# Gated linear attention in a fused decoder block: block-diagonal state tiles, and the order of state update and output copy on the vector engine

## The chip, the cores and the metric

The kernel runs on one core of a Trainium2 chip. The core has a matrix engine (TensorE; PE in the profile, PEld its weight loads), a vector engine (VectorE, DVE), a scalar engine (ScalarE, ACT), GpSimd (POOL) and a queue engine for transfers (SyncE, SP). The metric is the device time of one execution in microseconds (us); the kernel before takes 2816.35 us in the median of three runs.

## The reference, cut to what matters

The kernel computes one decoder block over 2048 tokens of width 1024: a mixing stage (two head groups side by side, mLSTM and gated linear attention), cross-attention and an MLP, all in float32. The change is in the gated linear attention (GLA), which has 4 heads with keys of 64 and values of 128 channels:

```python
def gla_chunkwise(q, k, v, log_a):
    # S_t = diag(a_t) S_{t-1} + k_t v_t^T, o_t = q_t S_t
    def step(Sst, inp):
        qc, kc, vc, la = inp
        b = jnp.cumsum(la, axis=2)
        diff = jnp.where(causal[:, :, None], b[:, :, :, None, :] - b[:, :, None, :, :], -jnp.inf)
        A = jnp.einsum('bhtd,bhsd,bhtsd->bhts', qc, kc, jnp.exp(diff))
        o = (jnp.einsum('bhts,bhse->bhte', A, vc)
             + jnp.einsum('bhtd,bhde->bhte', qc * jnp.exp(b), Sst))
        bL = b[:, :, -1]
        kw = kc * jnp.exp(bL[:, :, None] - b)
        S_new = jnp.exp(bL)[..., None] * Sst + jnp.einsum('bhsd,bhse->bhde', kw, vc)
        return S_new, o
```

The output of a chunk has a part from inside the chunk (A times v) and a part carried by the state (q exp(b) times S). The state of a head is a 64 x 128 matrix.

## The kernel before, in words

The tokens are taken in four groups of 512 (the first three in a loop, the last written out), each of four chunks of 128. Within a group every engine walks the same list of steps s, one for each slab of weights (128 rows by 512 columns). A product with weights is split in three terms of high and low parts, so a slab is 12 matmuls of TensorE (L1981). ACT rounds a slab to its high part (`w_hi`, L905), DVE subtracts to get the low part (`w_lo`, L1419), TensorE waits for `slab_lo`. Between the slabs stand the small operations of the two attentions, at steps fixed by hand (`M_SLAB` = 25, `G_SLAB` = 41). Each engine runs its own list in order, and semaphores join them.

The GLA part of a group takes steps 41 to 53. Chunk c, counted from 0, has three steps beginning at 41 + 3c:

- In the first step TensorE runs `levels(c, (0, 1))` (L2097, L2100), in the second `side_even_heads` (L2109), `levels(c, (2, 3))` and `side_odd_heads`. `levels` makes the sums inside a chunk, in 64 x 64 tiles of the array; for each head DVE masks the result (L1564, signals `lvl_masked`) and sums it (L1568). `levels(c, (2, 3))` waits until DVE has masked heads 0 and 1 of the same chunk.
- In the first step of the chunk after it (steps 44, 47, 50, 53), ahead of that chunk's `levels`, TensorE finishes chunk c: `outputs_start` multiplies the weighted queries `qe` of heads 0 and 2 by the state `stS` (L2135); `state_step` makes the update of the state (L2166, signals `s_full`); `outputs` does heads 1 and 3 of the carried part (L2135), after a wait for its own first pair (`o_even`), and adds the part from inside the chunk (L2157, signals `o_full`).
- At the same steps DVE copies the output out of PSUM (L1744, waits for `o_full`, signals `o_out`), updates the state (two instructions, L1749, one for each pair of heads, waits for `s_full`), and goes on to the masks of the next chunk.

The state tile `stS` is 128 partitions by 2 by 128: heads 0 and 2 lie on partitions 0 to 63, heads 1 and 3 on partitions 64 to 127, each pair j in its own columns. So L2135 is a matmul over 64 rows, two for each pair of partitions, and both pairs add into the same bank of PSUM (`work[:, 2]`).

ACT waits at the same steps for `o_out`, squares the output head by head (L1226), and then goes on: at step 47 it loads a table and applies the sigmoid of the gate (L1240) before the next rounding L905; at step 53 it scales the turned mLSTM heads (L1099, `x_hi`), whose low part DVE makes (L1585, `x_lo`) for the first slab of the output projection, step 56. At step 49 DVE gates the four mLSTM heads (`gate_heads`, L1606, 16 instructions).

DVE and ACT instructions may start on a part of the partitions: L1632 subtracts on partitions 64 to 87 (`gT[low]`), L1625 clears partitions 64 to 127 of `a_full`.

The lines that say what a sentence can't:

```python
for hd in hds:                       # carried(c, hds), L2131 to L2137
    j, p0 = hd // 2, 64 * (hd % 2)
    ins = mm(work[:, 2, cut[hd]], qe[p0:p0 + 64, c % 2, j, :], stS[p0:p0 + 64, j, :],
             start=(hd == 0), stop=False, skip_group_check=True)
```

## Time and profile before

| | |
|---|---|
| median of 3 runs | 2816.35 us (2816.01 to 2817.10) |
| time of the profiled execution | 2816.63 us |
| its span, first to last instruction | 2815.1 us |
| granted TensorE clock, mean | 0.999 |
| TensorE busy | 2796.2 us (99%) |
| DVE busy | 1812.2 us (64%) |
| ACT busy | 1514.2 us (54%) |
| share of TensorE in the chain that ended last | 98% |

Columns of the timeline rows below: start in us from the span's start, time in us from the first start to the last end of the row, engine, line, operation, output and inputs by the program's names, shapes, number of instructions in the row, and in brackets idle time of the engine before it and what ended it. A float32 matmul shows as two records. The span of 1.1 us less than the profiled time is the part around the program. A busy matrix engine is not one that waits for nothing: ends of matmuls are modelled, and only the distance from start to start shows its pace.

### The profile page before, as it was taken

What the parts mean: (1) busy time and instruction counts of PE and PEld (TensorE: products, weight loads), DVE (VectorE), ACT (ScalarE), POOL (GpSimd) and SP (SyncE); (2) the same over time, 40 slices, a digit from 0 to 9 for tenths busy, and PEclk for the clock granted to TensorE, in tenths of its full rate; (3) what the DMA queues carried; (4) which work ended last, traced back from release to release, by engine and by line L of the source; (5) the groups of instructions that cost most, each with busy time, mean ns of one, the idle gap of its engine ahead of it and who ended that gap; (6) DMA issues with size and microseconds to landing.
All of it is one profiled execution on the core that took longest, in us unless ns stands there. A gap on an engine that the chain in (4) does not pass through costs nothing.

```text
span 2815.1 us, 44964 instructions
## 1 busy us (share of the span) xinstructions
PE 2796.2 (99%) x15076; PEld 2328.2 (83%) x15076; DVE 1812.2 (64%) x3011; ACT 1514.2 (54%) x3126; POOL 1054.5 (37%) x1334
## 2 busy tenths in 40 slices
PE   8999999999999999999999999999999999999998
PEld 8888888888878888888888888888888888888887
DVE  6376764776686755556788675466668675545665
ACT  6555444566655444555565544456655544455553
POOL 5264554665354400234546320044435550013330
PEclk9999999999999999999999999999999999999999
DMA  6732476565552222355554222255455222234442
GB/s 216 251 105 67 173 268 242 186 211 151 149 188 83 76 89 90 108 171 161 164 177 135 69 84 90 90 158 179 143 150 199 81 74 90 90 104 144 151 149 83
DMA packets 185906, 393.41 MB, mean 140 GB/s; under 512 B 14224, under 2 KB 14368, under 8 KB 185664
## 3 DMA queue, kind: packets, MB, share of 16 engines
q1 hardware_dynamic: 160112, 309.89, 35.2%
q0 software_dynamic: 22880, 75.72, 8.0%
q10 hardware_dynamic: 2672, 4.76, 0.5%
q8 instruction: 129, 2.11, 0.3%
q14 instruction: 113, 0.93, 0.1%
HBM read 346.24 MB, written 33.59 MB: 135 GB/s over the span
## 4 chain that ended last, share of the span: by engine, by line
PE 98%; DMA 1%; ACT 0%; DVE 0%; issue 0%; POOL 0%; ACTq 0%; DVEq 0%
PE bank L1981 44%; PE work L1981 22%; PE bank L2348 17%; PE work L2348 3%; PE work L1995 1%; PE bank L2386 1%; PE work L2097 1%; DMA vo_dram<-folded 1%; PE bank L1995 1%; PE work L2135 1%; PE work L2157 1%; PE work L2043 1%; PE work L2246 1%; PE work L2250 1%; PE work L2245 1%; PE work L2229 1%
## 5 line engine op out<-in xcount | busy, mean ns | idle before, releaser
L905 ACT ACTIVATE w_hi<-raw 128x512 fp32r<-128x512 f32 x1156 | 724.7, 630 | 1012.6 <-PE bank L1981 514.5
L1419 DVE TENSOR_TENSOR w_lo<-raw,w_hi 128x512 fp32r<-128x512 f32 x657 | 481.2, 736 | 785.8 <-ACT w_hi L905 784.2
L1417 DVE SCALAR_TENSOR_TENSOR w_lo<-raw,w_hi 128x512 fp32r<-128x512 f32 x499 | 448.8, 921 | 92.6 <-ACT w_hi L905 91.6
L737 POOL TENSOR_TENSOR hr<-qk 128x256 f32<-128x256 f32 x60 | 44.9, 750 | 773.3 <-ACT qk L1293 773.3
L2348 PE MATMUL bank<-w_hi,h_hi 128*128 128x512 f32 x720 | 280.3, 389 | 0.1
L2348 PE MATMUL bank<-w_hi,h_lo 128*128 128x512 f32 x720 | 280.1, 389 | 0.0
L2348 PE MATMUL bank<-w_lo,h_hi 128*128 128x512 f32 x720 | 280.1, 389 | 0.0
L1981 PE MATMUL bank<-w_hi,x_hi 128*128 128x512 f32 x640 | 255.2, 399 | 0.0
L1981 PE MATMUL bank<-w_lo,x_hi 128*128 128x512 f32 x640 | 249.6, 390 | 0.0
L1981 PE MATMUL bank<-w_hi,x_lo 128*128 128x512 f32 x640 | 249.5, 390 | 0.0
L727 POOL TENSOR_TENSOR h_lo<-qk,h_hi 128x256 fp32r<-128x256 f32 x180 | 180.7, 1023 | 71.1 <-ACT h_hi L1306 71.1
L1981 PE MATMUL work<-act_hi,w_hi 128*128 128x512 f32 x512 | 199.2, 389 | 0.0
L1981 PE MATMUL work<-act_lo,w_hi 128*128 128x512 f32 x512 | 199.2, 389 | 0.0
L1981 PE MATMUL work<-act_hi,w_lo 128*128 128x512 f32 x512 | 199.2, 389 | 0.0
L1981 PE MATMUL bank<-act_hi,w_hi 128*128 128x512 f32 x464 | 180.8, 390 | 0.0
L1981 PE MATMUL bank<-act_hi,w_lo 128*128 128x512 f32 x464 | 180.5, 389 | 0.0
L1981 PE MATMUL bank<-act_lo,w_hi 128*128 128x512 f32 x464 | 180.5, 389 | 0.0
L2348 PEld LDWEIGHTS bank<-w_hi,h_hi 128*128 128x128 f32 x720 | 135.1, 188 | 28.8 <-issue 0.7
L2348 PEld LDWEIGHTS bank<-w_hi,h_lo 128*128 128x128 f32 x720 | 135.1, 188 | 28.2
L2348 PEld LDWEIGHTS bank<-w_lo,h_hi 128*128 128x128 f32 x720 | 135.1, 188 | 27.9
L791 POOL TENSOR_TENSOR zz<-zz,gqkv 128x128 f32<-128x128 f32 x224 | 118.0, 564 | 106.8 <-ACT gqkv L1251 106.8
L1981 PE MATMUL bank<-x_hi,w_hi 128*128 128x512 f32 x384 | 152.9, 398 | 0.0
(405 smaller groups left out, 6465.0 us busy)
## 6 DMA issues: line engine op xcount, KB each, us to landing
raw<-in_w_dram SPq DMA_DIRECT2D x226, 512.0 KB, 3.9
raw<-sums_dram SPq DMA_DIRECT2D x120, 512.0 KB, 3.9
raw<-in_w_in_dram SPq DMA_DIRECT2D x112, 512.0 KB, 3.5
raw<-in_w_out_dram SPq DMA_DIRECT2D x32, 512.0 KB, 4.1
raw<-kq_dram SPq DMA_DIRECT2D x32, 512.0 KB, 3.8
raw<-vo_dram SPq DMA_DIRECT2D x32, 512.0 KB, 3.8
xres<-in_x_dram POOLq DMA_DIRECT2D x16, 512.0 KB, 5.9
early_rows<-in_w_dram POOLq DMA_DIRECT2D x8, 1024.0 KB, 8.8
```

Source lines behind the costliest of these rows:

```text
L727: nc.gpsimd.tensor_tensor(operand(q, h_lo)[:, kt, :], src, operand(q, h_hi)[:, kt, :].bitcast(F32), ALU.subtract).then_inc(operand_lo_pool, 1)
L737: nc.gpsimd.tensor_tensor(diff[:, kt, :], quarter(0, 0, kt), quarter(0, 1, kt), ALU.subtract).then_inc(diff_ready, 1)
L791: ins = nc.gpsimd.tensor_tensor(v[:, :, :, r, :], v[:, :, :, r, :], src, ALU.mult)
L905: nc.scalar.activation(w_hi[:, slot, :], raw[:, pair_slot, slot % 2, :], ACT.Copy).then_inc(slab_hi, 1)
L1417: ins = stt(out=w_lo[:, slot, :], in0=src, scalar=1.0, in1=hi, op0=ALU.mult, op1=ALU.subtract)
L1419: ins = tt(w_lo[:, slot, :], src, hi, ALU.subtract)
L1981: ins = mm(dst, left, right, start=(kt == 0 and j == 0), stop=(kt == KT - 1 and j == 2))
L1995: ins = transpose(into[kt % 4][:, i * P:(i + 1) * P], src[:, i, kt * P:(kt + 1) * P], ident[:])
L2043: ins = mm(wbank[2 + j % 2][:, hh * MEM:(hh + 1) * MEM], left, right, start=(k == 0 and i == 0), stop=(k == 1 and i == 2))
L2097: ins = mm(dst, z, z, start=True, stop=True)
L2135: ins = mm(work[:, 2, cut[hd]], qe[p0:p0 + 64, c % 2, j, :], stS[p0:p0 + 64, j, :], start=(hd == 0), stop=False, skip_group_check=True)
L2348: ins = mm(dst[:], left[:, kt, here], right[:, kt, :], start=(CHAIN_BEFORE[q] is None and kt == 0 and j == 0), stop=(kt == HALF - 1 and j ...
```

## The change

- The state tile becomes 128 partitions by 2 by 256, block-diagonal: of pair j, the even head's 64 x 128 block stands on partitions 0 to 63 in columns 0 to 127, the odd head's on partitions 64 to 127 in columns 128 to 255; the rest stays zero.
- So one matmul over all 128 rows makes the carried output of both heads of a pair (128 x 128 by 128 x 256). Both are issued in a row in `outputs_start`; the semaphore `o_even` and the second call of `carried` go.
- DVE updates the state before the output's copy, in four instructions on 64 partitions each, in the order of the heads: partitions 0, 64, 0, 64.
- Nine small tiles of four columns become one tile of ten rows, and the unused tile shrinks from 232 to 8 columns to make room.

```diff
-        stS = sb("stS", [P, 2, HD])
+        stS = sb("stS", [P, 2, 2 * HD])
...
                     if slot == 0 and 1 <= c <= NCH:
-                        dve.wait_ge(o_full, 4 * g + c)
-                        nc.vector.tensor_copy(tok[:, c - 1, COLS:], work[:, 2, :]).then_inc(o_out, 1)
                         dve.wait_ge(s_full, 4 * g + c)
                         if c >= 2:
                             dve.wait_ge(s_ready, 4 * g + c - 1)
-                        for j in range(2):
-                            ins = stt(out=stS[:, j, :], in0=stS[:, j, :], scalar=eb[:, (c - 1) % 2, j, CH - 1:CH],
-                                      in1=work[:, 3, j * HD:(j + 1) * HD], op0=ALU.mult, op1=ALU.add)
+                        for hd in range(HEADS):
+                            j, k, half = hd // 2, hd % 2, slice(64 * (hd % 2), 64 * (hd % 2) + 64)
+                            own = stS[half, j, k * HD:(k + 1) * HD]
+                            ins = stt(out=own, in0=own, scalar=eb[half, (c - 1) % 2, j, CH - 1:CH],
+                                      in1=work[half, 3, j * HD:(j + 1) * HD], op0=ALU.mult, op1=ALU.add)
                         ins.then_inc(s_ready, 1)
+                        dve.wait_ge(o_full, 4 * g + c)
+                        nc.vector.tensor_copy(tok[:, c - 1, COLS:], work[:, 2, :]).then_inc(o_out, 1)
...
-                def carried(c, hds):
-
-                    for hd in hds:
-                        j, p0 = hd // 2, 64 * (hd % 2)
-                        ins = mm(work[:, 2, cut[hd]], qe[p0:p0 + 64, c % 2, j, :], stS[p0:p0 + 64, j, :],
-                                 start=(hd == 0), stop=False, skip_group_check=True)
-                    return ins
+                def carried(c, j):
+
+                    return mm(work[:, 2, j * 2 * HD:(j + 1) * 2 * HD], qe[:, c % 2, j, :], stS[:, j, :],
+                              start=(j == 0), stop=False, skip_group_check=True)
...
                     stand_alone(pe)
-                    carried(c, (0, 2)).then_inc(o_even, 1)
+                    for j in range(2):
+                        carried(c, j)
...
                     pe.wait_ge(at_full, 4 * g + c + 1)
-                    pe.wait_ge(o_even, 4 * g + c + 1)
                     stand_alone(pe)
-                    carried(c, (1, 3))
```

On TensorE, where a chunk is finished (here at step 47), the order was as follows. The rows give the stationary operand's columns by the moving one's; `stS`, `kwT` and `sg` are the state, the turned weighted keys and the weights inside the chunk.

```order
L1981 MATMUL bank<-w_hi,x_lo 128x512
L2135 MATMUL work<-stS,qe 128x128 [waits o_out,o_ss]
L2135 MATMUL work<-stS,qe 128x128
L2166 MATMUL work<-gqkv,kwT 64x128 [waits side_out]
L2166 MATMUL work<-gqkv,kwT 64x128 x3
L2135 MATMUL work<-stS,qe 128x128 [waits at_full,o_even]
L2135 MATMUL work<-stS,qe 128x128
L2157 MATMUL work<-gqkv,sg 128x128 x4
```

With the change it is:

```order
L1975 MATMUL bank<-w_hi,x_lo 128x512
L2127 MATMUL work<-stS,qe 128x256 [waits o_out,o_ss]
L2127 MATMUL work<-stS,qe 128x256
L2156 MATMUL work<-gqkv,kwT 64x128 [waits side_out]
L2156 MATMUL work<-gqkv,kwT 64x128 x3
L2147 MATMUL work<-gqkv,sg 128x128 [waits at_full]
L2147 MATMUL work<-gqkv,sg 128x128 x3
```

Four matmuls of 128 columns over 64 rows became two of 256 columns over 128 rows, all of them ahead of the state's update.

On DVE, at steps 49 and 50, the order was:

```order
L1606 SCALAR_TENSOR_TENSOR qk<-tok,hscale,qk 128x128 x15
L1414 REGISTER_ALU
L1419 TENSOR_TENSOR w_lo<-raw,w_hi 128x512 [waits slab_hi]
L1744 COPY tok<-work 128x512 [waits o_full]
L1749 SCALAR_TENSOR_TENSOR stS<-stS,eb,work 128x128 [waits s_ready,s_full]
L1749 SCALAR_TENSOR_TENSOR stS<-stS,eb,work 128x128
L1562 REGISTER_ALU
L1564 TENSOR_TENSOR mw<-work,lvl_mask 128x448 [waits lvl_full]
```

With the change it is:

```order
L1598 SCALAR_TENSOR_TENSOR qk<-tok,hscale,qk 128x128 x15
L1406 REGISTER_ALU
L1411 TENSOR_TENSOR w_lo<-raw,w_hi 128x512 [waits slab_hi]
L1741 SCALAR_TENSOR_TENSOR stS<-stS,eb,work 64x128 [waits s_ready,s_full]
L1741 SCALAR_TENSOR_TENSOR stS<-stS,eb,work 64x128 x3
L1745 COPY tok<-work 128x512 [waits o_full]
L1554 REGISTER_ALU
L1556 TENSOR_TENSOR mw<-work,lvl_mask 128x448 [waits lvl_full]
```

The copy moved behind the state's update, and the update has four instructions instead of two, in front of the next mask in both.

## Rows read from the trace of the kernel before

**Rows 1.** The page: busy time, share of the span and instructions of each engine.
```profile
PE 2796.2 (99%) x15076; PEld 2328.2 (83%) x15076; DVE 1812.2 (64%) x3011; ACT 1514.2 (54%) x3126; POOL 1054.5 (37%) x1334
```

**Rows 2.** Timeline of PE at step 44 of the first group.
```profile
265.07 0.39 PE L1981 MATMUL bank<-w_hi,x_lo 128*128 128x512 f32 x1
265.39 0.71 PE L2135 MATMUL work<-stS,qe 64*128 64x128 f32 x4
266.03 0.66 PE L2166 MATMUL work<-gqkv,kwT 128*64 128x128 f32 x8
266.62 0.71 PE L2135 MATMUL work<-stS,qe 64*128 64x128 f32 x4
267.26 1.16 PE L2157 MATMUL work<-gqkv,sg 128*128 128x128 f32 x8
268.35 0.93 PE L2097 MATMUL work<-zz 64*64 64x64 f32 x48
```

**Rows 3.** Timeline of PE in the mLSTM part: from a slab into float32 matmuls.
```profile
223.65 0.39 PE L1981 MATMUL bank<-w_hi,x_lo 128*128 128x512 f32 x1
223.88 1.05 PE L2229 MATMUL work<-qk 128*128 128x128 f32 x8
224.76 0.60 PE L2233 MATMUL work<-ident,qk 128*128 128x128 f32 x4
```

**Rows 4.** Timeline of PE: `levels` of steps 47 and 48, 50 and 51.
```profile
282.86 0.93 PE L2097 MATMUL work<-zz 64*64 64x64 f32 x48
...
286.99 0.28 PE L2097 MATMUL work<-zz 64*64 64x64 f32 x3
...
297.37 0.93 PE L2097 MATMUL work<-zz 64*64 64x64 f32 x48
...
301.76 0.93 PE L2097 MATMUL work<-zz 64*64 64x64 f32 x48
```

**Rows 5.** Timeline of DVE, steps 48 to 51.
```profile
288.76 0.69 DVE L1419 TENSOR_TENSOR w_lo<-raw,w_hi 128x512 fp32r<-128x512 f32 x1 [1.57 <-ACT w_hi L905]
...
298.37 0.68 DVE L1744 COPY tok<-work 128x512 f32<-128x512 f32 x1
298.97 0.59 DVE L1749 SCALAR_TENSOR_TENSOR stS<-stS,eb,work 128x128 f32<-128x128 f32 x2
299.49 0.61 DVE L1564 TENSOR_TENSOR mw<-work,lvl_mask 128x448 f32<-128x448 f32 x1
...
301.00 0.62 DVE L1564 TENSOR_TENSOR mw<-work,lvl_mask 128x448 f32<-128x448 f32 x1
```

**Rows 6.** DVE busy in one window: its ends, length, busy time, instructions, clock, transfers.
```profile
288.76:301.62 12.86, 12.75 (x29) 1.00 0.26 83
```

**Rows 7.** Timeline of DVE in the second group: an instruction on partitions 64 to 87.
```profile
799.84 0.67 DVE L1419 TENSOR_TENSOR w_lo<-raw,w_hi 128x512 fp32r<-128x512 f32 x1
...
800.54 0.69 DVE L1632 TENSOR_TENSOR gT<-work,gT 24x512 fp32r<-24x512 f32 x1
```

**Rows 8.** Timeline of DVE: a clearing of partitions 64 to 127.
```profile
248.53 1.13 DVE L1618 SCALAR_TENSOR_TENSOR stC<-stC,bc,work 128x129 f32<-128x129 f32 x4
249.76 0.27 DVE L1625 MEMSET sg<- 64x256 f32 x1
```

**Rows 9.** Timeline of DVE at step 44: the output's copy.
```profile
268.45 0.69 DVE L1744 COPY tok<-work 128x512 f32<-128x512 f32 x1 [1.60 <-PE work L2157]
```

**Rows 10.** Timeline of ACT, steps 47 and 48.
```profile
284.86 1.28 ACT L1240 ACT_TABLE_LOAD   x1
286.15 2.07 ACT L1240 ACTIVATE qk<-bank 128x512 f32<-128x512 f32 x4
288.08 0.65 ACT L905 ACTIVATE w_hi<-raw 128x512 fp32r<-128x512 f32 x1
```

**Rows 11.** Timeline of DVE at step 54: the last low parts before the output projection.
```profile
318.35 1.42 DVE L1585 SCALAR_TENSOR_TENSOR x_lo<-tok,norm_g,x_hi 128x512 fp32r<-128x512 f32 x2 [0.20 <-ACT x_hi L1099]
```

**Rows 12.** Timeline of PE at step 56: the output projection's first matmul.
```profile
320.22 0.39 PE L1981 MATMUL work<-w_hi,x_hi 128*128 128x512 f32 x1
```

More of the change, by code:

```diff
@@ L111 @@
 PRO_ROWS = MEM // P + NCH
-SPARE = 232
+SPARE = 8
 N_SUMS = HB * HALF
@@ L217, in program @@
         stC = sb("stC", [P, HEADS, HD + 1])
-        stS = sb("stS", [P, 2, HD])
+        stS = sb("stS", [P, 2, 2 * HD])
         mrow = sb("mrow", [1, NCH + 1, HEADS])
-        ss = sb("ss", [P, NCH])
-        ss_b = sb("ss_b", [P, NCH])
-        var = sb("var", [P, NCH])
-        lnv = sb("lnv", [P, NCH])
-        y0 = sb("y0", [P, NCH])
-        y1 = sb("y1", [P, NCH])
-        rstd = sb("rstd", [P, NCH])
-        rs_attn = sb("rs_attn", [P, NCH])
-        rs_mlp = sb("rs_mlp", [P, NCH])
+        row_cols = sb("row_cols", [P, 10, NCH])
+        ss, ss_b, var, lnv, y0, y1, rstd, rs_attn, rs_mlp = (row_cols[:, k, :] for k in range(9))
         hss = sb("hss", [P, 2, NCH, HEADS])
@@ L402, in program @@
         at_full = sem("at_full")
-        o_even = sem("o_even")
         o_full = sem("o_full")
```

## The prediction

> **What bounds the kernel now.** I read the page first. TensorE is busy 99% of the span, DVE 64% [rows 1], so the kernel is TensorE's instruction stream, and a change pays by what it takes out of that stream, unless it makes TensorE wait. Then I read TensorE's timeline where a chunk is finished, from start to start. After the last matmul of a slab at 265.07 come the four L2135 records of heads 0 and 2 at 265.39, the state's update at 266.03, the four records of heads 1 and 3 at 266.62, the inner part at 267.26, and `levels` at 268.35 [rows 2]: 3.28 us for the whole passage. Last I asked who is close behind TensorE. In steps 47 and 48 the two calls of `levels` start 4.13 us apart, in steps 50 and 51 4.39 us [rows 4], though the same work stands between them: TensorE waits there for 0.26 us, once in each group. It waits for DVE's mask of head 1, which ends at 301.62 (301.00 + 0.62), and goes on at 301.76 [rows 4, 5]. DVE has no room there: from 288.76 to 301.62, 12.86 us, it is busy for 12.75 [rows 6]. So at this one place of the group DVE is the bound already, and the change gives DVE more to do.
>
> **What TensorE gains.** In one shape of the array, a float32 record with 128 moving columns takes 0.11 us from start to start (eight from 223.88 to 224.76), and the first starts 0.23 after a slab's last matmul [rows 3], which is the slab's own pace. The four L2135 records take 0.64 instead of 0.44, and the first starts 0.32 after the slab instead of 0.23 [rows 2]. So a passage from one tile shape (128x128, 64x128, 128x64) to another costs about 0.20 us, half as a late start, half on the first record behind it. Before there are four such passages up to L2157: slab to 64x128, to 128x64, to 64x128, to 128x128. After there are two. The removed wait for `o_even` costs nothing: the passage from the second L2135 to L2157, with no wait in it, costs as much as the one into it. The streaming stays the same, eight records of 0.11 against four with 256 columns. No row has a float32 record of 256 columns. It lies between twice 0.11, 0.22, and a slab's record, 0.23, which I read as streaming as long; I take 0.22, since the overhead of one record is in both. New passage: 0.23 + 3 x 0.22 + (0.22 + 0.09) + 0.59 for the state (266.03 to 266.62) + 1.09 for the inner part (267.26 to 268.35) = 2.88 us. Gain 0.40 us for each chunk (0.36 at the other bound), 16 chunks, 6.4 us if nothing else moves.
>
> **What DVE pays.** Two updates of 128 partitions become four of 64. Their time goes by the columns, which stay 128: 0.59 for two that overlap, that is 0.26 from start to start and 0.33 for the last [rows 5]. If the four overlapped in the same way they would add 2 x 0.26 = 0.52 us. But they jump between partition 0 and partition 64. Where DVE now goes on to partitions 64 to 87, the instruction before ends at 800.51 and the next starts at 800.54 [rows 7], 0.03 after it; instructions in a row on the same partitions start 0.08 before the end of the one ahead (the copy ends at 299.05, the update starts at 298.97) [rows 5]. The clearing of partitions 64 to 127 starts 0.10 after the last end (248.53 + 1.13 = 249.66, then 249.76) [rows 8]. So I price an update behind one on other partitions at its 0.34 plus 0.03, 0.37 from start to start, and the copy behind them the same way: 4 x 0.37 = 1.48 us from the first update to the copy. The lower bound is 4 x 0.26 = 1.04 (no such gap), the upper 4 x 0.45 = 1.80 (a gap of 0.11, rounded up from the clearing's). I take 0.37 as its row is an arithmetic instruction with two inputs, one from PSUM, as here, and repeats in each group. Before, the updates held the next mask back by 0.52 (298.97 to 299.49); after it is 1.48, 0.96 more.
>
> The Trainium skill, VectorE: DVE Perf Modes, section "Two Vector instructions with no wait between them", speaks against this change: an instruction whose operand starts in another quadrant of partitions than the last one's starts only when all earlier ones have finished. By that rule updates two, three and four and the copy would each be held, as priced from rows above. With the rule the sum below comes out; without it the first rival does.
>
> **Where it matters.** Moving the update forward uses time in which DVE had stood idle, for 1.60 us before the copy [rows 9]. The new `s_full` lands at 265.30 + 0.66 + 0.31 + 0.66 = 266.93, so the copy can start at 266.97 + 1.48 = 268.45. That is where it starts now [rows 9], although `o_full` comes 0.40 earlier. So in steps 44, 47 and 53 the copy stays where it is relative to the start of the passage, and what hangs on the copy gains nothing from that chunk. The mask behind it no longer has the update in front, and starts earlier than now. One group then goes like this (time against before, negative is a gain):
>
> - Step 44: TensorE -0.40. DVE keeps up.
> - Step 47: TensorE -0.80 in all. The copy has only the -0.40 of step 44. On it hang ACT's squares, the table load at 284.86, the sigmoids at 286.15, the rounding at 288.08 [rows 10] and DVE's split at 288.76, which waited for that rounding [rows 5]. So the filled stretch of DVE starts only 0.40 earlier.
> - Step 50: DVE comes from the gating without a pause, so `s_full` is no limit; its block is 0.96 longer. The mask of head 1 is at -0.40 + 0.96 = +0.56, and TensorE, which came at -1.20, waits for it. From here all stands at +0.56.
> - Step 53: TensorE -0.40 again, +0.16. The copy has none of it, so `x_lo`, complete at 319.77 (318.35 + 1.42) [rows 11], stays, while the first matmul that needs it, at 320.22 [rows 12], wants to come at 319.82 and its weights one record, 0.23, sooner. I put 0.15 for that wait (0 to 0.23): +0.31.
>
> Four groups: 4 x 0.31 = 1.2 us more. Everything else costs nothing. Merging the nine small tiles changes no instruction; the semaphore and its wait stood beside running matmuls; the small matmuls are fewer. ACT and POOL do the same work. Their cover is that TensorE's other steps find their slabs split well ahead, and the change takes none of it away: after step 53 the work is as before.
>
> The sum is made against the profiled execution, 2816.63 us, which becomes 2817.9; it is 0.28 above the median, to which I apply the same difference: 2816.35 + 1.2 = **2817.6 us**.
>
> **The rivals.**
>
> - *No gap on DVE (chance 0.15).* Updates overlap at 0.26. The copy then follows `o_full` and moves with TensorE, so step 47's gain reaches DVE too: -0.80 + 0.52 = -0.28 at step 51, -0.68 after step 53, -2.7 us in all, 2813.6. The distance of starts in a row [rows 5] speaks for it, the start on partition 64 [rows 7] against.
> - *DVE has room at step 50 (0.06).* If the 0.26 us of wait [rows 4] were something else than the mask, TensorE would keep its 6.4 us: 2810.0. The filled window [rows 6] speaks against it.
> - *The gap is long, and the time ends higher (0.12).* At 0.45 for each update the copy is 0.32 later in steps 47 and 53 too. Then the stretch starts at -0.08, its block is 1.80 - 0.52 = 1.28 longer, the mask is at +1.20, step 53 gives +0.80, the wait before the projection grows to 0.47: +1.27 a group, 5.1 us in all, 2821.5. It decides from a gap above the 0.03 us of [rows 7] on; the clearing [rows 8] speaks for it. Past a gap of 0.12 it is a real slowdown.
> - *The wide matmul doesn't pass as two halves (0.05).* If a record of 256 columns took 0.23 or more, or the passage into it still cost 0.20, TensorE would gain only 0.36 or 0.20 in steps 44 and 53; the rest is DVE's anyway. Worth 0.3 to 1.6 us on top of the forecast: 2817.9 to 2819.2.
>
> **How the numbers follow.** The forecast has 0.62. A measurement of this kernel can tell about 0.2%, 5.6 us, from no change: below 2810.7 is faster, above 2822.0 slower. Only the second rival reaches the first, only the third (at a longer gap yet) the second. The range is 2812.8 to 2821.0: it takes in the forecast with its bounds, the first and fourth rivals and the lower part of the third. Faster 0.06, no difference 0.89, slower 0.05.
>
> **What would show it.** In the timeline after: the passage from the slab's last matmul to `levels` at 2.88 us instead of 3.28; four updates 0.37 apart; the copy of step 44 still about 3.38 us behind the slab's last matmul; the copy of step 50 about 1.5 us behind its first update; the two `levels` of steps 50 and 51 about 6.15 us apart instead of 4.39 (the first at -1.20, the second at +0.56); those of steps 47 and 48 still 4.13. If updates are 0.26 apart, or the two `levels` of steps 50 and 51 stay within 5.3 us, as in the first rival (-1.20 and -0.28), the forecast is wrong.

## The result, and the profile after

| | before | after |
|---|---|---|
| median, same session | 2817.10 us (2815.43 to 2820.92, 9 runs) | 2822.77 us (2819.61 to 2827.99, 9 runs) |
| ratio | | 1.0021 (95% interval 1.0012 to 1.0030) |
| profiled execution, its span | 2816.63 us, 2815.1 | 2822.39 us, 2820.9 |
| granted clock, mean | 0.999 | 0.998 (mean of the nine runs 0.997) |

The change costs 5.9 us by the ratio; forecast were 1.2 us, and a range to 2821.0. Before's median is 2816.6 to 2821.5 us from one session to another, so below only ratios are compared, each with before's runs of its own session.

The page of the kernel after answers to [rows 1]:

```profile
PE 2795.1 (99%) x15012; PEld 2327.5 (83%) x15012; DVE 1826.1 (65%) x3043; ACT 1512.7 (54%) x3126; POOL 1052.9 (37%) x1334
```

TensorE is busy 1.1 us less in a span that is 5.8 us longer. The averages hide the rest. Its timeline at step 44, against [rows 2], and at steps 50 to 52, against [rows 4]:

```profile
264.64 0.39 PE L1975 MATMUL bank<-w_hi,x_lo 128*128 128x512 f32 x1
264.87 1.02 PE L2127 MATMUL work<-stS,qe 128*128 128x256 f32 x4
265.82 0.66 PE L2156 MATMUL work<-gqkv,kwT 128*64 128x128 f32 x8
266.41 1.16 PE L2147 MATMUL work<-gqkv,sg 128*128 128x128 f32 x8
267.50 0.93 PE L2091 MATMUL work<-zz 64*64 64x64 f32 x48
...
295.62 0.93 PE L2091 MATMUL work<-zz 64*64 64x64 f32 x48
...
301.89 0.93 PE L2091 MATMUL work<-zz 64*64 64x64 f32 x48 [1.91 <-DVE mw L1556]
...
305.06 0.63 PE L1975 MATMUL bank<-w_hi,x_lo 128*128 128x512 f32 x1
305.48 0.63 PE L1975 MATMUL bank<-w_hi,x_hi 128*128 128x512 f32 x1
305.91 0.62 PE L1975 MATMUL bank<-w_lo,x_hi 128*128 128x512 f32 x1
...
307.30 0.39 PE L1975 MATMUL bank<-w_hi,x_hi 128*128 128x512 f32 x1
307.53 0.40 PE L1975 MATMUL bank<-w_lo,x_hi 128*128 128x512 f32 x1
```

Two things are to be seen. The passage of step 44 takes 2.86 us (264.64 to 267.50) instead of 3.28, and the two `levels` of steps 50 and 51 start 6.27 us apart instead of 4.39, the second behind a wait of 1.91 us. And behind that wait the matmuls of a slab start 0.43 us apart, then again 0.23: the same instruction at half the pace. The windows of the kernel after say why (columns: ends, length, busy time and instructions of PE, PEld, DVE, ACT, POOL, then granted TensorE clock, transfers):

```profile
300.00:302.00 2.00, 0.11 (x6) 0.14 (x9) 1.93 (x4) 1.30 (x8) 2.00 (x4) 1.00 1.00 293
302.00:304.00 2.00, 2.00 (x62) 1.52 (x61) 1.97 (x4) 0.00 (x0) 2.00 (x4) 0.74 0.53 109
304.00:306.40 2.40, 2.40 (x7) 1.88 (x7) 2.28 (x3) 0.65 (x2) 2.40 (x5) 0.50 0.54 113
```

TensorE stands for nearly all of 300 to 302; then the granted clock is 0.50, its 1.2 GHz level, for 3.41 us, from 303.0 to 306.4. Such a stretch is called a fall below. There is one in the second group too (0.60 and 0.62 in two windows that each hold a part of it) and one in the fourth, but none in the third. In the trace of before no group has one; its windows at the same place:

```profile
302.00:304.00 2.00, 2.00 (x64) 1.65 (x56) 1.97 (x4) 0.48 (x3) 2.00 (x4) 1.00 0.65 144
304.00:306.40 2.40, 2.40 (x12) 1.92 (x12) 2.23 (x3) 0.23 (x1) 2.40 (x5) 1.00 0.56 120
```

(Its mean clock of 0.999 comes from the last 5 us of the execution, behind TensorE's last matmul, where the clock is 0.50 in every kernel here.) On DVE, against [rows 5]:

```profile
296.85 0.68 DVE L1411 TENSOR_TENSOR w_lo<-raw,w_hi 128x512 fp32r<-128x512 f32 x1
297.46 1.42 DVE L1741 SCALAR_TENSOR_TENSOR stS<-stS,eb,work 64x128 f32<-64x128 f32 x4
298.91 0.69 DVE L1745 COPY tok<-work 128x512 f32<-128x512 f32 x1
299.63 0.62 DVE L1556 TENSOR_TENSOR mw<-work,lvl_mask 128x448 f32<-128x448 f32 x1
...
301.12 0.62 DVE L1556 TENSOR_TENSOR mw<-work,lvl_mask 128x448 f32<-128x448 f32 x1
```

The updates hold the copy back for 1.45 us, and the mask that TensorE waits for ends at 301.74.

### The profile page after: what moved, and what is told of

It reads as the page before. It is cut to its first block, busy times and chain, and to the rows that moved or that the text cites. A ratio compares the mean times of both kernels' runs of the same rounds, so it can differ in the third digit from the quotient of the medians.

```text
span 2820.9 us, 44868 instructions
## 1 busy us (share of the span) xinstructions
PE 2795.1 (99%) x15012; PEld 2327.5 (83%) x15012; DVE 1826.1 (65%) x3043; ACT 1512.7 (54%) x3126; POOL 1052.9 (37%) x1334
## 4 chain that ended last, share of the span: by engine, by line
PE 97%; DVE 2%; issue 1%; ACT 1%; DMA 0%; DVEq 0%; ACTq 0%
PE bank L1975 43%; PE work L1975 22%; PE bank L2338 17%; PE work L2338 3%; PE work L1989 1%; PE bank L2376 1%; PE bank L1989 1%; PE work L2037 1%; PE work L2091 1%; PE bank L2059 1%; PE work L2236 1%; PE work L2240 1%; PE work L2219 1%; PE work L2235 1%; DVE qk L1598 0%
```

## The experiments

Theory 1: the change gains 0.41 us in each of 16 passages (the chunk's end, from the slab to `levels`) and loses it where DVE is late, at step 51; the wait there is long enough for the clock to fall behind it, and each fall costs some 1.4 us more. The rival: the clock falls because of the matmuls themselves, two of full rows in a row, or the change costs something elsewhere.

### Updates that are not held, and the copy on ACT

```diff
-                            j, k, half = hd // 2, hd % 2, slice(64 * (hd % 2), 64 * (hd % 2) + 64)
+                            j, k, half = hd // 2, hd % 2, slice(0, 128)
```

> The changed kernel, but each of the four state updates works on all 128 partitions instead of 64 (so the zero blocks of the state fill up; only the time is of use). Theory 1 (DVE's order sets the time, and a long wait of TensorE at step 51 makes its clock fall): the updates no longer jump between partition 0 and 64, so they start 0.26 us apart, the copy comes 0.41 us earlier in steps 47 and 53, the wait at step 51 shrinks from 1.9 us to about 1.2, and with an unbroken clock the time is about 2.7 us under before; each fall of the clock adds about 1.4 us. Rival (the jumps cost nothing, the loss comes from the wide matmuls or their heat on the clock): updates as far apart as in the change, and as many stretches at 0.5 of the clock as in the change.

Each update works on all rows, so the zero blocks fill up and the output is not the block's; only the time counts. Measured: ratio 0.9985 (0.9976 to 0.9994), -4.2 us, clock 1.00 in all groups. The second kernel takes DVE's copy away and lets ACT make it ahead of its squares:

```diff
-                        act.wait_ge(o_out, 4 * g + c)
+                        act.wait_ge(o_full, 4 * g + c)
+                        nc.scalar.activation(tok[:, c - 1, COLS:], work[:, 2, :], ACT.Copy).then_inc(o_out, 1)
...
-                        dve.wait_ge(o_full, 4 * g + c)
-                        nc.vector.tensor_copy(tok[:, c - 1, COLS:], work[:, 2, :]).then_inc(o_out, 1)
```

> The changed kernel, but ACT makes the output's copy instead of DVE, right after the matmuls; state update and matmuls as in the change. Theory 1: copy follows TensorE again, DVE's block at step 50 is 0.34 us longer than before the change instead of 0.95, the wait at step 51 is about 1.0 us, the time about 3.4 us under before if the clock holds. Rival (wide matmuls bring the clock down): the stretches at 0.5 stay, and the time stays at or above that of before.

Measured: 2810.87 us, ratio 0.9973 (0.9962 to 0.9983), -7.6 us: faster than both kernels, and more than the 3.4 us that were expected. The wait was 0.6 us and not 1.0, and `levels` stood 4.94 us apart; 16 x 0.41 less 4 x 0.55 are 4.4 us. The profiled executions' spans differ by 5.1 us (2810.0 against 2815.1), which is near the lower end of the interval; what the ratio has above that no trace shows. From the list of TensorE's waits, first of the kernel after, then of the first and of the second experiment (columns: total us, times, longest):

```profile
PE work L2091 <- DVE mw L1556: 5.7, 3, 1.9
PE work L2091 <- issue: 2.0, 1, 2.0
```
```profile
PE work L2091 <- DVE mw L1556: 3.3, 6, 1.0
PE work L2091 <- issue: 1.0, 1, 1.0
```
```profile
PE work L2090 <- DVE mw L1557: 1.9, 4, 0.6
PE work L2090 <- issue: 0.5, 1, 0.5
```

Both kernels have the change's wide matmuls, and no group of either has a fall: behind waits of 1.0 and 0.6 us the clock stayed at 1.00. The rival needs another cause for that.

### Queries padded instead of the state

GpSimd makes the queries with zeros in the other head's rows; the state stays compact, with two full updates, and four matmuls of 128x128 by 128 columns replace the two wide ones.

```diff
+                    nc.gpsimd.tensor_tensor(qe(c)[:, 1], qe(c)[:, 0],
+                                            halves[:, 1:2].unsqueeze(2).to_broadcast([P, 2, CH]),
+                                            ALU.mult).then_inc(pad_step, 1)
+                    pool.wait_ge(pad_step, 8 * g + 2 * c + 2)
+                    nc.gpsimd.tensor_tensor(qe(c)[:, 0], qe(c)[:, 0],
+                                            halves[:, 0:1].unsqueeze(2).to_broadcast([P, 2, CH]),
+                                            ALU.mult).then_inc(kq_ready, 1)
...
-                        ins = mm(work[:, 2, cut[hd]], qe[p0:p0 + 64, c % 2, j, :], stS[p0:p0 + 64, j, :],
+                        ins = mm(work[:, 2, cut[hd]], qe(c)[:, hd % 2, hd // 2, :], stS[:, hd // 2, :],
```

> Another way to the same gain on TensorE: the state stays compact (two updates on all partitions, moved ahead of the copy), and GpSimd makes two copies of the weighted queries with the other half of the partitions zero, so that four matmuls over all 128 rows with 128 columns take the place of the two with 256. Theory 1: TensorE's passage is as short as in the change (about 2.88 us), the copy follows o_full, the wait at step 51 is about 0.66 us, no fall of the clock, about 4.8 us under before. Rival (the full-row matmuls themselves bring the clock down or DVE does not matter): as slow as the change.

> The padded queries with compact state, and ACT makes the output's copy. Theory 1: DVE's block at step 50 is 0.6 us shorter than before, no wait at step 51 (the 0.26 us of before go too), the whole gain of TensorE stands: about 7.5 us under before, no stretch at 0.5. Rival: clock falls as in the change, time near before.

Measured: 0.9998 (0.9989 to 1.0007) and 0.9992 (0.9983 to 1.0001), both misses: 0.5 and 2.3 us less than before by the ratios, neither clear of no change. The passage of step 44 took 2.88 us, 0.40 less, as wanted, but DVE was late at step 51 all the same. Its sixteen gates of step 49 took 4.28 us in the kernel before and 5.06 in the third experiment, where GpSimd's two new products stand beside the first of them:

```profile
291.12 0.95 POOL L810 TENSOR_TENSOR tok<-tok,halves 128x256 f32<-128x256 f32 x1
...
291.52 5.06 DVE L1625 SCALAR_TENSOR_TENSOR qk<-tok,hscale,qk 128x128 f32<-128x128 f32 x16
...
292.15 0.61 POOL L814 TENSOR_TENSOR tok<-tok,halves 128x256 f32<-128x256 f32 x1
```

The whole 0.78 us falls on the first two gates, 0.70 and 0.77 us long instead of 0.34; the fourteen behind them start 0.26 us apart, as before. It is so in all four groups of both kernels. TensorE waited 1.2 us for the mask in the third experiment and 0.4 in the fourth (clock 1.00 behind it), 1.4 and 1.7 us for `x_lo` in the last group, and once ahead of a group's first matmuls, 2.0 us up to 1461.6 and 2.1 us up to 1459.7, where the clock then was 0.50 for 3.41 us. Why `x_lo` was late there is open. The other wait is no mark of these kernels: at the same place the other traces have 0.2 to 2.65 us, the longest in the eleventh experiment, whose GpSimd does what it did before. And the mean clocks of the two kernels' runs, 0.9990 and 0.9991, are that of before: most of their executions have no fall.

### The wait without the change

Only at step 50, sums over the PSUM bank (two, then three) are put ahead of the output's copy of the kernel before:

```diff
+                        if c == 3:
+                            for k in range(2):
+                                nc.vector.tensor_reduce(spare[:, k:k + 1], work[:, 2, :], AX.X, ALU.add)
                         nc.vector.tensor_copy(tok[:, c - 1, COLS:], work[:, 2, :]).then_inc(o_out, 1)
```

> The kernel before, with nothing of the change in it, and two more DVE instructions (sums over a PSUM bank into a spare column, which nothing reads) ahead of the output's copy in step 50 of each group only: 2 x 0.69 = 1.37 us. TensorE's wait ahead of the levels of step 51 becomes 0.26 + 1.37 = 1.6 us in each group. Theory 1 (the long wait itself brings the clock down, whatever matmuls the kernel has): 4 x 1.4 = +5.5 us by the waits alone, up to +11 us if 1.6 us is already long enough for the clock to fall to 0.50 after each. Rival (the full-row matmuls of the change bring it down): +5.5 us, and the clock stays at 1.00, for this and for the next kernel.

> As the kernel before this one, with three such DVE instructions: TensorE's wait at step 51 becomes 0.26 + 3 x 0.69 = 2.3 us, longer than the 1.9 us after which the clock fell in three of four groups of the changed kernel. Theory 1: the clock falls to 0.50 for 3.4 us after the wait in all four groups, +4 x (2.06 + 1.4) = +13.8 us. Rival (the change's matmuls bring it down): the clock stays at 1.00 and the time grows by the waits alone, +8.2 us.

Measured: 1.0018 (1.0008 to 1.0027), +5.1 us, and 1.0044 (1.0029 to 1.0060), +12.4 us. The sums overlap and took 0.60 us each from start to start, so `levels` of steps 50 and 51 stood 5.55 and 6.14 us apart and the waits were 1.15 and 1.65 us, shorter than the 1.6 and 2.3 that were expected. In the traces the clock fell behind them in one and in two of four groups. Windows of the kernel with two sums, third group, and timeline of the one with three, second group:

```profile
1648.00:1650.00 2.00, 2.00 (x7) 1.63 (x6) 1.93 (x4) 0.65 (x2) 2.00 (x4) 0.52 0.50 107
```
```profile
977.18 0.93 PE L2100 MATMUL work<-zz 64*64 64x64 f32 x48 [1.65 <-DVE mw L1564]
...
980.18 0.63 PE L1984 MATMUL bank<-w_hi,x_hi 128*128 128x512 f32 x1
980.61 0.63 PE L1984 MATMUL bank<-w_lo,x_hi 128*128 128x512 f32 x1
```

Neither has a matmul of the change. For the three sums, four waits longer by 1.75 us are 7.0 us; the rest of the 12.4 is 5.4, between three and four falls an execution. The trace has two; the mean clock of its four runs, 0.99725 against 0.9991 of before, says 0.00187 x 2832 / 1.7 = 3.1 (a fall is 3.41 us at half, 1.7 us of full clock). So a longer wait is enough to bring the clock down, and the rival falls. The kernel with two sums carries little of this: four waits longer by 1.16 us are 4.6 of its 5.1 us, and the mean clock of its ten runs, 0.9992, is that of before, so the one fall of its trace is the exception.

### DVE's half alone

```diff
-                        for j in range(2):
-                            ins = stt(out=stS[:, j, :], in0=stS[:, j, :], scalar=eb[:, (c - 1) % 2, j, CH - 1:CH],
-                                      in1=work[:, 3, j * HD:(j + 1) * HD], op0=ALU.mult, op1=ALU.add)
+                        for hd in range(HEADS):
+                            j, half = hd // 2, slice(64 * (hd % 2), 64 * (hd % 2) + 64)
+                            own = stS[half, j, :]
+                            ins = stt(out=own, in0=own, scalar=eb[half, (c - 1) % 2, j, CH - 1:CH],
+                                      in1=work[half, 3, j * HD:(j + 1) * HD], op0=ALU.mult, op1=ALU.add)
```

> The kernel before with DVE's half of the change alone: four updates of 64 partitions in place of two of 128, in the state's old compact layout, still behind the output's copy; TensorE unchanged. By the changed kernel's row an update on other partitions than the one before is held, 0.365 us from start to start, so the updates take 1.46 us in place of 0.52, +0.94 us ahead of the masks. Theory 1: waits of some 0.3 us before the levels of steps 45 and 48 and of 0.9 to 1.2 us at step 51, which the clock survives: +4 to +6 us over the kernel before, clock 1.00. Rival (a jump of partitions costs DVE nothing, four instructions of 0.26 us take 1.04): +0.5 x 4 = +2 us or less.

Measured: 1.0030 (1.0019 to 1.0041), +8.5 us, clock 1.00. `levels` of steps 45 and 48 came 0.33 us late each and of step 51 0.65 later than before, 1.3 us a group as expected; what was not expected is the first line here, 0.6 us a group ahead of step 56:

```profile
PE work L1983 <- DVE x_lo L1585: 2.4, 4, 0.7
PE work L2099 <- DVE mw L1564: 1.9, 3, 0.6
```

Together 4 x 1.3 + 2.4 = 7.6. The direction was right (4 to 6 us were expected), the size too small by the second place where DVE is close behind TensorE.

### Other orders on DVE

> The changed kernel with one thing moved: of the 16 products of head and gate that DVE does in step 49, the eight of heads 2 and 3 (2.15 us) go behind the masks of step 50. The updates and the copy stay as the change has them. Theory 1 (all that the change loses, it loses at the wait of step 51 and in the low clock behind it): the mask is there in time, the levels of steps 50 and 51 stand 4.1 us apart in place of 6.3, the clock stays at 1.00, and the 0.41 us gained in each of 16 passages stays: -5 to -7.5 us against the kernel before, unless the late heads make TensorE wait for x_lo at step 53 and later (then -3). Rival (the full-row matmuls or the held updates cost time elsewhere too): no faster than the kernel before by more than 2 us.

```diff
-                        gate_heads(0, HEADS)
+                        gate_heads(0, HEADS, range(2))
+                    if s == 50:
+                        gate_heads(0, HEADS, (2, 3))
```

Measured: 1.0060 (1.0046 to 1.0074), 17 us slower where 5 to 7.5 us less were expected: a miss. `levels` stood 4.20 us apart, the wait at step 51 was gone, and TensorE waited 4.5 us for `x_lo` instead:

```profile
PE work L1977 <- DVE x_lo L1577: 17.1, 4, 4.5
```

The clock fell in all four groups, for 3.41 us once and 6.83 three times, and three of these stretches began up to 1.8 us before the wait had ended. The gated heads go on to GpSimd's transfers and to ACT, and have no room.

> The changed kernel with one reordering on DVE, in step 50 of each group only: the first two masks with their sums go ahead of the four updates and the copy, in place of behind them. No instruction is added or taken away, and the gates of step 49, whose move behind the masks made x_lo late, stay. The mask that the levels of step 51 wait for then ends 1.46 + 0.69 = 2.15 us sooner. Theory 1 (the change lost its gain at that wait and in the low clock that follows it): levels of steps 50 and 51 4.1 us apart (6.3 in the changed kernel), clock 1.00, and 16 x 0.41 + 4 x 0.3 = 7.8 us less than the kernel before, some -5 to -8 us measured. Rival (x_lo of step 53 and later, or the updates that now come 1.9 us later, become the next wait, as the late gates did): the levels stand 4.1 us apart too, but TensorE waits for x_lo or for the state, and no more than 2 us is gained.

> The kernel with the output's copy on ACT (the second experiment), with the same reordering in step 50. There the wait at step 51 was 0.6 us, and the clock held. Theory 1: the 0.6 us go, 4 x 0.5 = -2 us against that kernel, -8 us against the kernel before, about the same as the kernel ahead of this one, since nothing more than the wait was to be had. Rival (ACT's copy late on a busy ACT delays w_hi or x_hi): slower than the kernel ahead of this one by 2 us or more.

```diff
+                    if s == 50:
+                        for k in range(2):
+                            level_sum(c, 2 * slot + k)
...
-                    if slot < 2 and 0 <= c < NCH:
+                    if slot < 2 and 0 <= c < NCH and s != 50:
```

Measured: 1.0027 (1.0016 to 1.0038) and 1.0002 (0.9993 to 1.0011), both misses, by 12 us or more and by 8. I had overlooked that ahead of these `levels` TensorE runs `side_even_heads` (L2106 here), which waits for `s_ready`: at step 51 it needs the updated state first. TensorE's timeline of the ninth experiment, and its DVE:

```profile
301.90 0.41 PE L2106 MATMUL work<-zz 64*64 64x64 f32 x4 [2.35 <-issue]
302.15 1.07 PE L2094 MATMUL work<-zz 64*64 64x64 f32 x48
```
```profile
300.38 1.42 DVE L1744 SCALAR_TENSOR_TENSOR stS<-stS,eb,work 64x128 f32<-64x128 f32 x4
```

The last update ends at 301.80, and TensorE goes on. The wait is 2.35 us (1.8 with the copy on ACT), and the clock fell in three groups (two). Updates and masks must both be done by step 51; only the copy need not.

> The changed kernel with its four updates in the order of heads 0, 2, 1, 3 in place of 0, 1, 2, 3, so that DVE jumps between halves of the partitions twice in a chunk and not at every update. If the hold of 0.365 us from start to start belongs to the jump, the starts stand 0.26, 0.365, 0.26 and 0.365 us apart, the copy starts 1.25 us behind the first update in place of 1.46, and the wait at step 51 is 1.7 us in place of 1.9: -0.2 x 4 = -0.8 us against the changed kernel, and the clock still falls in two or three groups. Rival (every update on 64 partitions is slow, or none follows another closer since each reads PSUM): 1.46 us as before and no gain.

```diff
-                        for hd in range(HEADS):
+                        for hd in (0, 2, 1, 3):
```

Measured: 0.9997 (0.9988 to 1.0006). Singly, the updates of step 44 start 0.265, 0.347, 0.271 and (to the copy) 0.384 us apart, where 0.26, 0.365, 0.26 and 0.365 were expected. At step 50:

```profile
296.66 1.23 DVE L1741 SCALAR_TENSOR_TENSOR stS<-stS,eb,work 64x128 f32<-64x128 f32 x4
297.92 0.69 DVE L1745 COPY tok<-work 128x512 f32<-128x512 f32 x1
```

1.26 us to the copy instead of 1.45. The wait was 1.5 us and the clock fell behind it in one group (and once behind a wait of 2.6 us elsewhere). By the ratios the kernel is 6.8 us faster than the changed one, not 0.8. `levels` 5.88 us apart instead of 6.27 are 1.6 us of it in four groups; the mean clock of its runs, 0.9980 against 0.9970, is 1.7 falls fewer, some 2.6 us at 1.5 to 1.6 us each. The rest is within the two intervals.

> The changed kernel with one part of the change undone: the output's copy goes back ahead of the four updates. TensorE's side stays as changed. Updates behind the copy end sooner at steps 44 and 47 relative to nothing that TensorE waits for: DVE idled ahead of the copy before. So the four updates, 1.46 us, stand behind a copy that starts when the output is full, and the masks of these steps end 0.9 us later than in the kernel before: waits of 0.3 us at steps 45 and 48, and about 1.3 to 1.9 us at step 51, where DVE is behind in either order. Theory 1: between -1 and +3 us against the kernel before, the clock falling in none to three groups according to that last wait. Rival (the order of copy and updates is what the change gains by): slower than the changed kernel by 3 us or more.

```diff
+                        dve.wait_ge(o_full, 4 * g + c)
+                        nc.vector.tensor_copy(tok[:, c - 1, COLS:], work[:, 2, :]).then_inc(o_out, 1)
                         dve.wait_ge(s_full, 4 * g + c)
...
```

(The copy's two lines go from behind the updates.) Measured: 1.0002 (0.9993 to 1.0011), the wait at step 51 1.1 us, clock 1.00, and 0.36 us at steps 45 and 48. The old order with the new matmuls is thus no slower than the kernel before, and faster than the full change. Up to step 51 a group is only 0.2 us shorter than the changed one (44.14 against 44.36), and it loses 0.6 us more to `x_lo` ahead of step 56; but TensorE has been made to wait at 45 and 48, comes some 0.7 us later to step 51, waits 1.1 us there instead of 1.9, and no fall follows. What the full change does wrong is to gather these waits in one.

### The copy out of the way

> The changed kernel with DVE's copy of the output behind the two masks of its step instead of ahead of them; the four updates stay ahead. TensorE needs the updated state and then the mask at step 51, the copy only before the carried product of step 53. Theory 1: the wait at step 51 goes from 1.9 to 1.9 - 0.69 = 1.2 us, the clock falls in none or one of four groups (0 of 4 at 1.1 us, 1 of 4 at 1.2 us so far), so 4 x 0.7 + 2.5 x 1.4 = 6 us less than the changed kernel, whose ratio was 1.0021: the kernel before within 2 us. Rival (ACT, which waits for that copy before its squares, comes late with w_hi, or TensorE waits for x_lo): no faster than the changed kernel, waits for w_lo, w_hi or x_lo in the list.

> The kernel ahead of this one with the updates in the order of heads 0, 2, 1, 3, which took 1.27 us to the copy in place of 1.46 in the eleventh experiment. Theory 1: the wait at step 51 is 1.0 us, the clock stays at 1.00 in all groups, 0.8 us less than the kernel ahead of this one and 1 to 3 us less than the kernel before. Rival: as for the kernel ahead.

In both the copy's two lines go behind the two masks of their step, in every chunk; the second has the order 0, 2, 1, 3 as well. Measured: 1.0047 (1.0033 to 1.0060) and 1.0051 (1.0038 to 1.0065): misses, with a fall in all four groups of both. Moved in every step, the copy of step 47 kept ACT waiting for 6.65 us ahead of its squares, and the sigmoid behind them came late for the bank that TensorE wanted. ACT's timeline, and a line of TensorE's waits, of the thirteenth experiment:

```profile
286.75 0.28 ACT L1218 ACTIVATE sg<-work 128x128 f32<-128x128 f32 x1 [6.65 <-DVE tok L1751]
...
289.20 2.06 ACT L1232 ACTIVATE qk<-bank 128x512 f32<-128x512 f32 x4
```
```profile
PE bank L1976 <- ACT qk L1232: 8.2, 4, 2.1
```

So it was moved at step 50 only, without and with the order 0, 2, 1, 3:

```diff
+                    if slot == 0 and 1 <= c <= NCH and s != 50:
                         dve.wait_ge(o_full, 4 * g + c)
                         nc.vector.tensor_copy(tok[:, c - 1, COLS:], work[:, 2, :]).then_inc(o_out, 1)
...
+                    if s == 50:
+                        dve.wait_ge(o_full, 4 * g + c)
+                        nc.vector.tensor_copy(tok[:, c - 1, COLS:], work[:, 2, :]).then_inc(o_out, 1)
```

> The changed kernel with DVE's copy of the output behind the two masks in step 50 only; in steps 44, 47 and 53 it stands where the change puts it. In the profiled run of the changed kernel the copy, 0.69 us, stood between the updates and the masks there. Theory 1: the wait at step 51 goes from 1.9 to 1.2 us, levels of steps 50 and 51 5.5 to 5.6 us apart in place of 6.27; the clock falls in none to two of four groups; 4 x 0.7 + 1 to 3 x 1.4 = 4 to 7 us less than the changed kernel (ratio 1.0021), so a ratio of 0.9995 to 1.0007. ACT's squares come 2.8 us later, with a rounding of w_hi behind them, as in the ninth experiment, where TensorE did not wait for it. Rival (whatever is moved on DVE in this stretch only makes another wait): 1.002 or more.

> As the kernel ahead of this one, with the updates in the order of heads 0, 2, 1, 3 as well. Theory 1: wait at step 51 of 1.0 us, levels 5.2 to 5.4 us apart, the clock stays at 1.00 in all or all but one group, 1 to 2 us less than the kernel ahead: a ratio of 0.9985 to 1.0. Rival: as for the kernel ahead, 1.001 or more.

Measured: 0.9997 (0.9988 to 1.0006) and 0.9990 (0.9981 to 0.9999), both inside the expectation. TensorE of the first of them:

```profile
300.39 0.93 PE L2095 MATMUL work<-zz 64*64 64x64 f32 x48 [1.15 <-DVE mw L1556]
```

The clock was 1.00 in both. The same instructions as the change, one copy once in a group 4.4 us behind the first update instead of 1.45, and its loss is gone.

> The second experiment (copy of the output on ACT, wait of 0.6 us at step 51, clock 1.00, ratio 0.9973) with the updates in the order 0, 2, 1, 3. Theory 1: the wait falls from 0.6 to 0.4 us or less, 4 x 0.2 = -0.8 us against that kernel, ratio 0.997 or a little lower, clock 1.00. Rival (something else than this wait ends last): the same time as the second experiment.

Measured: 0.9977 (0.9967 to 0.9987), `levels` 4.77 us apart instead of 4.94, clock 1.00. The 0.7 us are too few to be told from the second experiment's 0.9973; either is the best version found.

### The waits and the clock, put together

The waits are TensorE's idle time ahead of these `levels`; that of before is the 0.26 us by which its `levels` stand further apart there. The last column is worked out from the mean clock of all runs of the kernel: (0.9991 less that clock) x 2820 / 1.7, wherever in the execution the falls are.

| kernel | longest wait at step 51, us | groups of the trace with a fall behind it | falls an execution, by the runs' clock |
|---|---|---|---|
| before | 0.3 | 0 of 4 | 0 |
| padded queries, copy on ACT | 0.4 | 0 | 0 |
| copy on ACT in the order 0, 2, 1, 3; copy on ACT; DVE's half alone | 0.4; 0.6; 0.6 | 0 | 0.2; 0; 0 |
| copy late at 50 in the order 0, 2, 1, 3; without it | 0.9; 1.3 | 0 | 0; 0 |
| all rows; copy first; padded queries | 1.0; 1.1; 1.2 | 0 | 0; 0; 0.2 |
| before with two sums | 1.2 | 1 | 0 |
| updates in the order 0, 2, 1, 3 | 1.6 | 1 | 1.8 |
| before with three sums | 1.6 | 2 | 3.1 |
| masks first, copy on ACT | 1.8 | 2 | 2.1 |
| the change | 2.0 | 3 | 3.5 |
| masks first | 2.5 | 3 | 5.4 (falls of 6.83 us count as two) |

One trace each, so its counts are samples; the last column is of 4 to 11 executions. Both go with the wait at step 51 and not with the matmuls. At other places, and in the kernels that the table leaves out: four waits of 4.1 to 4.5 us each came with a fall, eleven of 2.0 to 2.65 us eight times, three of 1.7 to 1.8 us at step 51 each, but eight of 1.4 to 1.9 us ahead of step 0 or of step 56 never. So the place counts too. (The 7 us that every execution waits at its start are left out, since the clock's record begins behind them.)

## Why the prediction was wrong

- *TensorE's gain.* Forecast a passage of 2.88 us, measured 2.86; 0.41 us a chunk instead of 0.40. Right: a record of 256 columns takes 0.215, and two passages between tile shapes are saved.
- *DVE's price.* Forecast 0.37 from start to start and 1.48 us to the copy; measured 0.35 to 0.37 (0.385 to the copy) and 1.45. The rule of the Trainium skill, VectorE: DVE Perf Modes, section "Two Vector instructions with no wait between them", by which an instruction that starts in another quadrant of partitions than the one before starts only when that has finished, stood behind the forecast and against the first rival. The traces agree three ways: updates on all rows start 0.26 apart, those in the order 0, 2, 1, 3 start 0.27 apart where the rows stay and 0.35 where they change, those of the change 0.35 to 0.37 throughout.
- *The places.* Step 51 late by the mask, forecast `levels` 6.15 apart, measured 6.27; those of steps 47 and 48 stand 4.09 apart instead of the forecast's 4.13. From step 42 to step 51 a group took 44.36 us instead of 43.80: +0.56, the forecast's number for the mask.
- *The step that failed* is "From here all stands at +0.56", and with it "Everything else costs nothing". It priced the wait at step 51 by its length alone. It had the length right, had in front of it that TensorE would stand for 2.0 us (6.15 less 4.13) where it had stood for 0.26, and had no term for what TensorE does when it goes on. From `levels` of step 51 to step 53 the kernel before took 7.40, 7.38, 7.40 and 7.38 us in its four groups; after, 8.84, 8.76, 7.30 and 8.91. That is 4.3 us, of 5.8 in the span. Against the 7.30 us of its own third group, which has no fall and a shorter start of step 53's passage, the three falls cost 1.5 to 1.6 us each, 4.6 in all: what the forecast lacks. That the 1.2 us that stay are just the forecast's is in part luck, as the waits ahead of step 0 alone differ by a microsecond and more between the traces. The nine runs agree: their mean clock of 0.9970, against 0.9991 in the runs of before of the later sessions, is 5.9 us of full clock, 3.5 falls.
- *The small terms.* The wait for `x_lo` before step 56, forecast 0.15 us in each group, did not show; it did, at 0.6 to 0.7, in the two kernels with updates behind the copy. That the first-placed update saves the copy nothing at steps 44 and 47 held: the copy starts 3.35 us behind the slab's last matmul there, 3.38 before.
- *The rivals.* "The gap is long" gave 2821.5, close to the result, by a mechanism that did not happen: the gap was 0.01 to 0.03 us. What was missing among the rivals was one in which the new wait has a consequence of its own.

That the longer wait is the cause is shown by the kernel with three sums, which has nothing else of the change, and by the sixteenth and seventeenth experiments, which keep all of the change and shorten the wait; that the change gains when the wait is short, by the second, the fifteenth and (a little) the seventeenth. Why a wait of one length is followed by a fall in one group and not in the next stays open, and so does what else, beside the wait, differs between these groups.

## What to carry to other kernels

On a kernel that TensorE fills to 99%, a wait isn't priced by its length alone: read the granted clock behind the waits of similar length, or, if there are none, give a low clock a rival of its own. Here many small gains of TensorE, gathered into one wait on a late engine, were worse than the same waits left spread (the changed kernel against the twelfth experiment). Before moving work on a late engine, list for each piece who needs it and when, along each engine that stands behind it: here the state, the masks, the heads and the copy at step 47 were all needed soon, and only the copy at step 50 was free to move.

## What the hardware showed unasked

- Behind waits of TensorE of 1.5 to 2.65 us the granted clock was 0.50 for 3.41 us (6.83 at times) in some groups and not in others; of eighteen waits of 1.1 to 1.3 us one was followed by such a stretch, of the shorter ones none. Each 3.41 us cost 1.5 to 1.6 us here (`levels` of step 51 to step 53 in 8.76 to 9.00 us instead of 7.30 with the change's matmuls and 7.40 without).
- DVE instructions on 64 partitions take as long as on 128 (0.34 us for 128 columns), and a jump to other partitions costs 0.09 to 0.13 us of overlap: the next update starts 0.35 instead of 0.26 us behind the one ahead, the copy 0.385 instead of 0.26 to 0.30.
- Sixteen DVE gates took 5.06 instead of 4.28 us where GpSimd multiplied beside the first two: those two took 0.70 and 0.77 us instead of 0.34. The kernel before has it too, for a subtraction of low parts (L1419), which took 1.18 us beside GpSimd's product for `qe` instead of 0.69 elsewhere:

```profile
292.47 1.18 DVE L1419 TENSOR_TENSOR w_lo<-raw,w_hi 128x512 fp32r<-128x512 f32 x1
292.36 0.74 POOL L801 TENSOR_TENSOR qe<-eb,gqkv 128x256 f32<-128x256 f32 x1
```
